# Weight sums behind earlier up tiles on DVE, and every second low half of the product units on POOL

## The chip, the cores and the metric

The kernel runs on one core of a Trainium2 chip. The metric is the device time of one execution in microseconds (us), lower is better. The engines of the core run their own instruction streams and wait for each other by semaphores: TensorE (PE, the matmuls), VectorE (DVE), ScalarE (ACT), GpSimd (POOL), and SyncE (SP), whose queue issues most of the loads from HBM.

## What is computed

Two two-layer transformer-like blocks, one after the other, over 512 tokens of width 1024 in float32 (four layers, 0 to 3). Each layer has mixers and ends with a feed-forward part of inner width 4096, which is where the change is:

```python
h = rms_norm(x, norm_mlp[l])
x = x + jnp.square(jax.nn.relu(h @ w_mlp_in[l])) @ w_mlp_out[l]
```

## The kernel before

**Splits.** Every float32 matmul is made of three on rounded values: a weight unit of 128x1024 (`w_raw`) is copied to `w_hi` by ACT (`split_hi`, L335) in a rounded type, and what is left, `w_lo` = raw - `w_hi`, is subtracted by POOL (`split_lo`, L408) or by DVE (`split_lo_dve`, L356); `by_dve(u)` says which. PE then does `w_hi`·H, `w_lo`·H and `w_hi`·L (L464 to L466). Three slots (`WB` = 3) hold the units in turn, so ACT may split unit u once PE is through with unit u - 3.

**Feed-forward, four blocks of 1024 hidden columns.** Each block has eight *up tiles* (one unit, 24 matmuls of 512 columns each), whose sums lie in two PSUM banks in turn, `acc0` and `acc1`: tile k + 2 can't begin until DVE has evacuated tile k (L723). ACT squares the tile; DVE and ACT then make sums of its quarters (`x_sum`, L730), their rounded halves XH (ACT, L678) and rests XL (`low`, DVE, L736). In blocks 0 to 2 the down projection follows as a *product stage* in Strassen's manner: seven products A11, A12, S1, S4, S2, S3, A22 (`PRODUCTS`), each of two weight units, so units 0 to 13, with 12 matmuls each (L615 to L617; six for the product's tile t = 0, six for t = 1). Their weights are four `quads` of two halves, loaded by SP (`load_quad`, L379), or sums of them, which DVE makes (`w_sum`, L759): two halves each for S1, S3, S2 and A22. S1 and S2 have a place of their own (`w_sums` in the rows), S3 and A22 replace a quad. Block 3 has an ordinary down projection. There are three product stages in each of four layers, twelve in all.

**Taking products.** Each product lies in two PSUM banks and is added to `rows` by DVE when its second unit is done (`take`, L769, one addition each for t = 0 and 1). S4 continues in the banks of S1: PE waits for S1's addition of the same t before unit 6. S2 continues in A11's banks, S3 in S2's, A22 in S3's.

**What sets the order.** Everything is written out by hand in the code's order; each engine works its list in order. For DVE the list is the loop `for k in range(NK)` of `mlp_dve` (tile k: evacuate, sums and rests of x, weight sums, a `w_low`) and the list of `w_low(b, m)`, `take`, `low` and `w_sum` behind it, m being the unit. In the three blocks of layer 0 a `side` function puts some other vector operations behind tile 2 (L1419 to L1429). ACT splits the unit of tile k + 3 when tile k is done, so units 0, 1 and 2 of the stage are split behind tiles 5, 6 and 7.

Of the kernel before, what the change touches and what calls it, by code (L numbers as in the profile page):

```python
# [24 lines left out]
P = 128  # L25
# [4 lines left out]
DEPTH = 2  # L30
HD = 64
EPS = 1e-6
UNIT = 1024
# [57 lines left out]
HALVES = 2  # L91
# [2 lines left out]
W_QUAD = dict(A11=0, A12=1, S4=3, S3=2, A22=1)  # L94
W_EXTRA = dict(S1=0, S2=1)
W_SUM = dict(S1=0, S3=2, S2=4, A22=6)
X_SUM = dict(S3=0, S1=1, S2=2, S4=3)
BY_PAIR = ("A11", "A12", "S1", "S4")
SPLITS = 4 * len(BY_PAIR) + 3
# [3 lines left out]
MULS = HALVES * len(PRODUCTS)  # L103


def taken_after(name):

    return HALVES * (PRODUCTS.index(name) + 1)


def split_after(name, pair):
# [43 lines left out]
def mul_of(u):  # L155

    layer, _, group, _, _, _ = UNITS[u]
    if not group.startswith("mul"):
        return None
    b = int(group[3:])  # L160
    return layer * (FB - 1) + b, u - FIRST_MUL[layer, b]


RANK = []
# [10 lines left out]
def program(nc, given, out):  # L175
# [5 lines left out]
    with ctx:  # L181
# [155 lines left out]
        def by_dve(u):  # L337


            layer, j, group, _, _, _ = UNITS[u]  # L340
            return mul_of(u) is not None or (layer < DEPTH and j >= 2 and group in ("first_in", "late_in"))

        def wait_lo(eng, u):
            mine = by_dve(u)
            eng.wait_ge(lo_split_dve if mine else lo_split, sum(by_dve(x) == mine for x in range(u + 1)))
# [21 lines left out]
        def load_quad(layer, b, q):  # L367


            if b:  # L370
                before, g = FIRST_MUL[layer, b - 1], layer * (FB - 1) + b - 1
                wait_lo(sp, before + {0: 1, 3: 7, 2: 11, 1: 13}[q])
                if q in (0, 3):
                    sp.wait_ge(w_summed, 4 * HALVES * g + (2 if q == 0 else 6))
            elif q == 0:
                n = FIRST_TILE[layer, "out"] + NK - 1
                sp.wait_ge(acc_ready[n % 2], n // 2 + 1)
            for half in range(HALVES):
                sp.dma_start(quads[:, q, half, :],  # L379
                             (w1_in if layer < DEPTH else w2_in)[layer % DEPTH, QUADS_AT[layer, b] + HALVES * q + half, :, :])\  # L380
                    .then_inc(quad_loaded[q], 16)
# [6 lines left out]
        def load_weights(layer):  # L388


            for u, unit in enumerate(UNITS):
                if unit[0] == layer and u >= 2 and mul_of(u) is None:
                    load_unit(u)
                    for b in range(FB - 1):
                        if unit[2] == f"up{b}":
                            at = unit[5] - FIRST_TILE[layer, f"up{b}"]
                            for q in ({1: (0, 3, 2, 1)} if b else {3: (0,), 4: (2,), 5: (3,), 6: (1,)}).get(at, ()):
                                load_quad(layer, b, q)
                if unit[0:2] == (layer, 12) and layer + 1 < LAYERS:
                    load_vec(layer + 1)  # L400

        def split_lo(layer):
            for u, (of, _, _, nk, ntile, _) in enumerate(UNITS):
                if of != layer or by_dve(u):
                    continue
                w, raw = nk * ntile * P, w_raw[:, RANK[u] % 2, 0:nk * ntile * P]
                pool.wait_ge(hi_split, u + 1)
                pool.tensor_tensor(w_lo[:, u % WB, 0:w], raw, w_hi[:, u % WB, 0:w], ALU.subtract)\  # L408
                    .then_inc(lo_split, 1)
# [185 lines left out]
        def products_pe(g, layer, b, XH, XL):  # L595


            for i, name in enumerate(PRODUCTS):
                for half in range(HALVES):
                    pe.wait_ge(x_low, SPLITS * g + split_after(name, 2 * half + 1))  # L600
                    u = FIRST_MUL[layer, b] + HALVES * i + half
                    wait_lo(pe, u)
                    for t in range(2):
                        if half == 0 and name not in OPENS:
                            before = [x for x in PRODUCTS[:i] if PRODUCT_BANK[x] == PRODUCT_BANK[name]][-1]
                            pe.wait_ge(product_taken, MULS * g + taken_after(before) - 1 + t)
                        elif half == 0 and g:
                            before = [x for x in PRODUCTS if PRODUCT_BANK[x] == PRODUCT_BANK[name]][-1]
                            pe.wait_ge(product_taken, MULS * (g - 1) + taken_after(before) - 1 + t)
                        for kk in range(2):  # L610
                            k, c = 2 * half + kk, slice(t * P, t * P + P)
                            xh, xl = XH[:, X_SLOT[name], k, c], XL[:, X_SLOT[name], k, c]
                            wh, wl = w_hi[:, u % WB, kk * T:kk * T + T], w_lo[:, u % WB, kk * T:kk * T + T]
                            bank, ends = product_bank(name, t)[:, :], half == HALVES - 1 and kk == 1
                            pe.matmul(bank, xh, wh, start=(name in OPENS and k == 0), stop=False, skip_group_check=True)  # L615
                            pe.matmul(bank, xl, wh, start=False, stop=False, skip_group_check=True)  # L616
                            last = pe.matmul(bank, xh, wl, start=False, stop=ends, skip_group_check=True)  # L617
                        if half == HALVES - 1:
                            last.then_inc(product_ready, 1)
                        elif t == 1:  # L620
                            last.then_inc(mul_used, 1)
# [94 lines left out]
        def mlp_dve(layer, midH, midL, XH, XL, mid, rows, spare, y, sq, side=None):  # L716
# [22 lines left out]
            def w_low(b, m):  # L739
                if by_dve(FIRST_MUL[layer, b] + m):  # L740
                    split_lo_dve(FIRST_MUL[layer, b] + m)
# [16 lines left out]
                    dve.wait_ge(w_summed, n)  # L758
                dve.tensor_tensor(into, first, second, ALU.subtract).then_inc(w_summed, 1)  # L759

            def take(g, name):
                half, n = PRODUCT_TO[name]
                for t in range(2):
                    at = MULS * g + taken_after(name) - 2 + t
                    dve.wait_ge(product_ready, MULS * g + HALVES * PRODUCTS.index(name) + t + 1)
                    if at:
                        dve.wait_ge(product_taken, at)
                    into = rows[:, 2 * half + t, n * T:n * T + T]
                    dve.tensor_tensor(into, product_bank(name, t)[:, :], into, ALU.add).then_inc(product_taken, 1)  # L769

            for b in range(FB - 1):
                g = layer * (FB - 1) + b
                ups = Group(layer, f"up{b}")
                for k in range(NK):
                    ups.evacuate(part, 1)
                    pair = k // 2
                    if side and k == 2:
                        side((0, 1, 5)[b])
                    if k % 2 == 0:
                        x_sum(g, "S3", pair, "A11", "A21", ALU.subtract)  # L780
                        low(g, "A11", pair)
                    else:
                        x_sum(g, "S1", pair, "A21", "A22", ALU.add)
                        low(g, "A12", pair)
                        x_sum(g, "S2", pair, "S1", "A11", ALU.subtract)
                        x_sum(g, "S4", pair, "A12", "S2", ALU.subtract)
                        if k == NK - 1:
                            w_low(b, 2)
                        low(g, "S1", pair)
                        low(g, "S4", pair)  # L790
                    for name, half in {4: (("S1", 0),), 5: (("S1", 1), ("S3", 0)), 6: (("S3", 1), ("S2", 0))}.get(k, ()):
                        w_sum(g, b, name, half)
                    if k in (5, 6):
                        w_low(b, k - 5)
                w_low(b, 3)
                w_sum(g, b, "S2", 1)
                take(g, "A11")
                w_low(b, 4)
                low(g, "S2")
                w_low(b, 5)  # L800
                w_sum(g, b, "A22", 0)
                w_low(b, 6)
                take(g, "A12")
                take(g, "S1")
                w_low(b, 7)
                low(g, "S3")
                w_low(b, 8)
                w_sum(g, b, "A22", 1)
                w_low(b, 9)
                take(g, "S4")  # L810
                w_low(b, 10)
                take(g, "S2")
                w_low(b, 11)
                low(g, "A22")
                w_low(b, 12)
                take(g, "S3")
                w_low(b, 13)
                take(g, "A22")
# [1942 lines left out]
```

## Time and profile before

| | us |
|---|---|
| median of 3 runs | 3726.57 |
| lowest and highest run | 3726.5, 3732.81 |
| the profiled execution, its own time | 3722.24 |
| its span, first to last instruction | 3720.9 |

The page gives busy time of each engine, the chain of work that ended last, and groups of instructions with the idle time before them; the timelines give single instructions in order of time.

### The profile page before, as it was taken

How to read it: one execution, taken by the hardware profiler on the slowest of the kernel's cores; microseconds unless marked ns; L12 is line 12 of the kernel's file. 1: busy time of each engine (PE TensorE's matmuls, PEld its weight loads, DVE VectorE, ACT ScalarE, POOL GpSimd, SP SyncE). 2: the span in 40 equal slices, each digit the busy share in tenths (PEclk: the TensorE clock that was granted, in tenths of full speed). 3: DMA queues.
4: the chain of work that ended last, by engine and by line, in shares of the span. 5: the costliest groups of instructions: out<-in, count | busy, mean ns of one | idle time of the engine just before them, and what ended most of it. 6: DMA issues, size and time to landing. Idle time of an engine off the chain costs nothing.

```text
span 3720.9 us, 44944 instructions
## 1 busy us (share of the span) xinstructions
PE 3555.5 (96%) x17332; PEld 2727.8 (73%) x17332; DVE 2376.9 (64%) x3416; ACT 1581.1 (42%) x2654; POOL 963.2 (26%) x390
## 2 busy tenths in 40 slices
PE   8889999988999999999999999999999999999998
PEld 6547778854777877577777677787667777777777
DVE  6987777788777754523463687775543355368774
ACT  6464442546444333544333444422444433444442
POOL 0003223100322342132323232244123232332223
PEclk9999999999999999999999999999999999999999
DMA  4103222310322241021212232224112221223312
GB/s 134 43 12 119 91 91 69 93 50 12 115 95 91 63 149 59 29 80 56 80 62 72 61 130 91 80 90 146 41 46 71 65 76 61 69 74 125 114 57 80
DMA packets 80803, 291.94 MB, mean 78 GB/s; under 512 B 9648, under 2 KB 11088, under 8 KB 80080
## 3 DMA queue, kind: packets, MB, share of 16 engines
q1 hardware_dynamic: 77808, 278.03, 23.8%
q10 hardware_dynamic: 2784, 11.03, 0.9%
q8 instruction: 139, 2.28, 0.2%
q14 instruction: 72, 0.59, 0.1%
HBM read 284.84 MB, written 2.10 MB: 77 GB/s over the span
## 4 chain that ended last, share of the span: by engine, by line
PE 76%; DVE 17%; issue 4%; ACT 3%; DMA 0%; DVEq 0%; SPq 0%; ACTq 0%
PE acc L464 18%; PE acc L466 17%; PE acc L465 17%; DVE w_lo L356 3%; PE banks L615 2%; PE banks L616 2%; PE banks L617 2%; PE banks L921 2%; PE banks L970 2%; PE banks L1300 2%; PE banks L953 2%; DVE rows L769 1%; DVE quads L759 1%; DVE w_sums L759 1%; PE banks L2084 1%
## 5 line engine op out<-in xcount | busy, mean ns | idle before, releaser
L408 POOL TENSOR_TENSOR w_lo<-w_raw,w_hi 128x1024 fp32r<-128x1024 f32 x386 | 963.0, 2497 | 2730.9 <-ACT w_hi L335 2730.8
L335 ACT ACTIVATE w_hi<-w_raw 128x1024 fp32r<-128x1024 f32 x422 | 447.5, 1061 | 1080.7 <-PE acc L466 890.6
L464 PE MATMUL acc<-hH,w_hi 128*128 128x512 f32 x1776 | 729.1, 411 | 11.9 <-DVE sig L2472 6.6
L466 PE MATMUL acc<-hL,w_hi 128*128 128x512 f32 x1776 | 699.5, 394 | 0.0
L465 PE MATMUL acc<-hH,w_lo 128*128 128x512 f32 x1776 | 699.1, 394 | 0.0
L464 PEld LDWEIGHTS acc<-hH,w_hi 128*128 128x128 f32 x1776 | 338.1, 190 | 97.6 <-issue 26.3
L464 PE MATMUL acc<-H,w_hi 128*128 128x512 f32 x1024 | 403.2, 394 | 3.8 <-DVE L L528 3.8
L466 PE MATMUL acc<-L,w_hi 128*128 128x512 f32 x1024 | 399.0, 390 | 0.0
L465 PE MATMUL acc<-H,w_lo 128*128 128x512 f32 x1024 | 398.6, 389 | 0.0
L466 PEld LDWEIGHTS acc<-hL,w_hi 128*128 128x128 f32 x1776 | 337.4, 190 | 73.3
L465 PEld LDWEIGHTS acc<-hH,w_lo 128*128 128x128 f32 x1776 | 338.1, 190 | 68.1 <-issue 4.8
L615 PE MATMUL banks<-w_hi,XH 128*128 128x512 f32 x672 | 264.5, 394 | 32.0 <-DVE rows L769 12.8
L616 PE MATMUL banks<-w_hi,XL 128*128 128x512 f32 x672 | 261.9, 390 | 0.0
L617 PE MATMUL banks<-w_lo,XH 128*128 128x512 f32 x672 | 261.8, 390 | 0.0
L464 PEld LDWEIGHTS acc<-H,w_hi 128*128 128x128 f32 x1024 | 192.3, 188 | 45.3 <-DVE L L528 5.5
L466 PEld LDWEIGHTS acc<-L,w_hi 128*128 128x128 f32 x1024 | 192.3, 188 | 40.3
L465 PEld LDWEIGHTS acc<-H,w_lo 128*128 128x128 f32 x1024 | 192.4, 188 | 40.0 <-issue 1.0
L335 ACT ACTIVATE w_hi<-quads 128x1024 fp32r<-128x1024 f32 x120 | 127.3, 1061 | 164.6 <-PE banks L617 96.7
L615 PEld LDWEIGHTS banks<-w_hi,XH 128*128 128x128 f32 x672 | 126.1, 188 | 72.7 <-issue 46.1
L2472 DVE TENSOR_TENSOR sig<-acc,rstd 128x512 f32<-128x512 f32 x48 | 33.2, 691 | 207.1 <-PE acc L466 206.8
L1057 DVE TENSOR_REDUCE stat<-banks 128x1 f32<-128x512 f32 (+2 forms) x192 | 95.8, 541 | 107.5 <-PE banks L928 74.8
L2386 DVE TENSOR_TENSOR Z<-acc,rstd 128x512 f32<-128x512 f32 x80 | 55.2, 689 | 169.3 <-PE acc L466 169.3
(365 smaller groups left out, 5973.4 us busy)
## 6 DMA issues: line engine op xcount, KB each, us to landing
w_raw<-in_stream SPq DMA_DIRECT2D x422, 512.0 KB, 3.6
quads<-in_stream SPq DMA_DIRECT2D x96, 512.0 KB, 4.5
cw<-in_cmpw ACTq DMA_DIRECT2D x2, 2048.0 KB, 7.2
mixed<-in_cmpw ACTq DMA_DIRECT2D x2, 2048.0 KB, 12.6
x_tok<-in_x SPq DMA_DIRECT2D x2, 1024.0 KB, 7.4
out<-probsT SPq DMA_DIRECT2D x4, 512.0 KB, 4.0
stack<-Z ACTq DMA_DIRECT2D x8, 128.0 KB, 2.3
stack<-Z ACTq DMA_DIRECT2D x8, 127.8 KB, 2.5
```

The costliest lines, as they stand in the source:

```text
L335: act.activation(w_hi[:, u % WB, 0:w], raw, ACT.Copy).then_inc(hi_split, 1)
L356: dve.tensor_tensor(w_lo[:, u % WB, 0:w], raw, w_hi[:, u % WB, 0:w], ALU.subtract)\
L408: pool.tensor_tensor(w_lo[:, u % WB, 0:w], raw, w_hi[:, u % WB, 0:w], ALU.subtract)\
L464: pe.matmul(acc[n % 2][:, :], wh, H[:, k, :], start=(k == 0), stop=False)
L465: pe.matmul(acc[n % 2][:, :], wl, H[:, k, :], start=False, stop=False)
L466: last = pe.matmul(acc[n % 2][:, :], wh, Lo[:, k, :], start=False, stop=(k == nk - 1))
L615: pe.matmul(bank, xh, wh, start=(name in OPENS and k == 0), stop=False, skip_group_check=True)
L616: pe.matmul(bank, xl, wh, start=False, stop=False, skip_group_check=True)
L617: last = pe.matmul(bank, xh, wl, start=False, stop=ends, skip_group_check=True)
L759: dve.tensor_tensor(into, first, second, ALU.subtract).then_inc(w_summed, 1)
L921: last = pe.matmul(self.score_banks[h % 3][:, 0:m], w["q"][r, qt * P:(qt + 1) * P], w["k"][r, lo * P:hi * P], start=True, stop=True, skip_ ...
L1057: dve.tensor_reduce(top, bank, AX_X, ALU.max, negate=True).then_inc(up(self.max_ready), 1)
```

## The change

Three things change, in all twelve blocks with a product stage.

1. `by_dve` now gives DVE only the even product units; POOL subtracts `w_lo` of units 1, 3, 5, ... 13, with the same operands.
2. The weight sums stand elsewhere in DVE's list: `W_SUM_AT` puts S1's two halves behind the evacuation of tile 2, S3's first behind tile 3, S3's second and S2's first behind tile 4, and S2's second behind tile 6, in each case ahead of that tile's `x_sum`. Before, they stood at the end of tiles 4 (S1), 5 (S1, S3) and 6 (S3, S2), and S2's second behind `w_low(b, 3)`. A22's second half moves from before `w_low(b, 9)` to behind `take(g, "S4")`.
3. DVE takes A12's first half, S1's first, A12's second, S1's second, where it took both halves of A12 and then both of S1. `taken_after(name, t)` counts in that order.

With them SP's waits ahead of a quad's load name both halves' subtractions, and in a layer's first block the quads are loaded behind tiles 3 (two quads), 4 and 5 where it was 3, 4, 5 and 6.

```diff
+W_SUM_AT = {2: (("S1", 0), ("S1", 1)), 3: (("S3", 0),), 4: (("S3", 1), ("S2", 0)), 6: (("S2", 1),)}
-def taken_after(name):
-    return HALVES * (PRODUCTS.index(name) + 1)
+TAKEN = [("A11", 0), ("A11", 1), ("A12", 0), ("S1", 0), ("A12", 1), ("S1", 1)]
+TAKEN += [(name, t) for name in ("S4", "S2", "S3", "A22") for t in range(2)]
+def taken_after(name, t):
+    return TAKEN.index((name, t)) + 1
...
@@ by_dve
-            return mul_of(u) is not None or (layer < DEPTH and j >= 2 and group in ("first_in", "late_in"))
+            if mul_of(u) is not None:
+                return mul_of(u)[1] % HALVES == 0
+            return (layer < DEPTH and j >= 2 and group in ("first_in", "late_in"))
@@ load_quad
-                wait_lo(sp, before + {0: 1, 3: 7, 2: 11, 1: 13}[q])
+                for half in range(HALVES):
+                    wait_lo(sp, before + {0: 0, 3: 6, 2: 10, 1: 12}[q] + half)
@@ load_weights
-                            for q in ({1: (0, 3, 2, 1)} if b else {3: (0,), 4: (2,), 5: (3,), 6: (1,)}).get(at, ()):
+                            for q in ({1: (0, 3, 2, 1)} if b else {3: (0, 2), 4: (3,), 5: (1,)}).get(at, ()):
@@ split_lo (POOL)
-                w, raw = nk * ntile * P, w_raw[:, RANK[u] % 2, 0:nk * ntile * P]
+                if mul_of(u) is None:
+                    w, raw = nk * ntile * P, w_raw[:, RANK[u] % 2, 0:nk * ntile * P]
+                else:
+                    m = mul_of(u)[1]
+                    w, raw = UNIT, mul_raw(of, PRODUCTS[m // HALVES], m % HALVES)
@@ mlp_dve
+                    for name, half in W_SUM_AT.get(k, ()):
+                        w_sum(g, b, name, half)
                     if k % 2 == 0:
                         x_sum(g, "S3", pair, "A11", "A21", ALU.subtract)
...
-                    for name, half in {4: (("S1", 0),), 5: (("S1", 1), ("S3", 0)), 6: (("S3", 1), ("S2", 0))}.get(k, ()):
-                        w_sum(g, b, name, half)
                     if k in (5, 6):
                         w_low(b, k - 5)
                 w_low(b, 3)
-                w_sum(g, b, "S2", 1)
                 take(g, "A11")
...
-                take(g, "A12")
-                take(g, "S1")
+                take(g, "A12", (0,))
+                take(g, "S1", (0,))
+                take(g, "A12", (1,))
+                take(g, "S1", (1,))
                 w_low(b, 7)
                 low(g, "S3")
                 w_low(b, 8)
-                w_sum(g, b, "A22", 1)
                 w_low(b, 9)
                 take(g, "S4")
+                w_sum(g, b, "A22", 1)
                 w_low(b, 10)
```

Three places of DVE's list show it, in the last product block of layer 1 (its other blocks read alike); the lines of the changed kernel lie some 12 further down (L723, L730, L736, L759, L356, L769 are L735, L742, L748, L771, L363, L781). L723 is a tile's evacuation, L730 a sum and L736 a rest of x, L759 a weight sum, L356 a `w_lo`, L769 an addition. DVE before, from the evacuation of tile 2 to that of tile 4:

```order
L723 SCALAR_TENSOR_TENSOR hidden<-acc,rstd 128x512
L730 TENSOR_TENSOR yt<-hidden 128x256
L736 TENSOR_TENSOR XL<-hidden,XH 128x256
L723 SCALAR_TENSOR_TENSOR hidden<-acc,rstd 128x512
L730 TENSOR_TENSOR hidden<-hidden 128x256
L736 TENSOR_TENSOR XL<-hidden,XH 128x256
L730 TENSOR_TENSOR hidden<-hidden 128x256 x2
L736 TENSOR_TENSOR XL<-hidden,XH 128x256 x2
L723 SCALAR_TENSOR_TENSOR hidden<-acc,rstd 128x512
```

And the same stretch of the changed kernel:

```order
L735 SCALAR_TENSOR_TENSOR hidden<-acc,rstd 128x512
L771 TENSOR_TENSOR w_sums<-quads 128x1024 x2
L742 TENSOR_TENSOR yt<-hidden 128x256
L748 TENSOR_TENSOR XL<-hidden,XH 128x256
L735 SCALAR_TENSOR_TENSOR hidden<-acc,rstd 128x512
L771 TENSOR_TENSOR quads<-quads 128x1024
L742 TENSOR_TENSOR hidden<-hidden 128x256
L748 TENSOR_TENSOR XL<-hidden,XH 128x256
L742 TENSOR_TENSOR hidden<-hidden 128x256 x2
L748 TENSOR_TENSOR XL<-hidden,XH 128x256 x2
L735 SCALAR_TENSOR_TENSOR hidden<-acc,rstd 128x512
```

Three weight sums now stand ahead of the x sums of tiles 2 and 3. The second place, DVE before, from the evacuation of tile 6 to the last rests of tile 7:

```order
L723 SCALAR_TENSOR_TENSOR hidden<-acc,rstd 128x512
L730 TENSOR_TENSOR yt<-hidden 128x256
L736 TENSOR_TENSOR XL<-hidden,XH 128x256
L759 TENSOR_TENSOR quads<-quads 128x1024
L759 TENSOR_TENSOR w_sums<-quads,w_sums 128x1024
L356 TENSOR_TENSOR w_lo<-quads,w_hi 128x1024
L723 SCALAR_TENSOR_TENSOR hidden<-acc,rstd 128x512
L730 TENSOR_TENSOR hidden<-hidden 128x256
L736 TENSOR_TENSOR XL<-hidden,XH 128x256
L730 TENSOR_TENSOR hidden<-hidden 128x256 x2
L356 TENSOR_TENSOR w_lo<-quads,w_hi 128x1024
L736 TENSOR_TENSOR XL<-hidden,XH 128x256 x2
```

And in the changed kernel:

```order
L735 SCALAR_TENSOR_TENSOR hidden<-acc,rstd 128x512
L771 TENSOR_TENSOR w_sums<-quads,w_sums 128x1024
L742 TENSOR_TENSOR yt<-hidden 128x256
L748 TENSOR_TENSOR XL<-hidden,XH 128x256
L735 SCALAR_TENSOR_TENSOR hidden<-acc,rstd 128x512
L742 TENSOR_TENSOR hidden<-hidden 128x256
L748 TENSOR_TENSOR XL<-hidden,XH 128x256
L742 TENSOR_TENSOR hidden<-hidden 128x256 x2
L363 TENSOR_TENSOR w_lo<-quads,w_hi 128x1024
L748 TENSOR_TENSOR XL<-hidden,XH 128x256 x2
```

One weight sum stands there in place of two, ahead of tile 6's x sum, and the `w_lo` of unit 1 is gone to POOL; the one of unit 2 is still last but one. The third place, DVE before at the stage's begin, from the `w_lo` of unit 3 to the additions of A12 and S1:

```order
L356 TENSOR_TENSOR w_lo<-quads,w_hi 128x1024
L759 TENSOR_TENSOR w_sums<-quads,w_sums 128x1024
L769 TENSOR_TENSOR rows<-banks,rows 128x512 x2
L356 TENSOR_TENSOR w_lo<-w_sums,w_hi 128x1024
L736 TENSOR_TENSOR XL<-hidden,XH 128x1024
L356 TENSOR_TENSOR w_lo<-w_sums,w_hi 128x1024
L759 TENSOR_TENSOR quads<-quads,w_sums 128x1024
L356 TENSOR_TENSOR w_lo<-quads,w_hi 128x1024
L769 TENSOR_TENSOR rows<-banks,rows 128x512 x4
```

And in the changed kernel, from the additions of A11 on:

```order
L781 TENSOR_TENSOR rows<-banks,rows 128x512 x2
L363 TENSOR_TENSOR w_lo<-w_sums,w_hi 128x1024
L748 TENSOR_TENSOR XL<-hidden,XH 128x1024
L771 TENSOR_TENSOR quads<-quads,w_sums 128x1024
L363 TENSOR_TENSOR w_lo<-quads,w_hi 128x1024
L781 TENSOR_TENSOR rows<-banks,rows 128x512 x4
```

The `w_lo` of units 3 and 5 and S2's sum are gone from it. The four additions at the end read alike, but their order is A12, S1, A12, S1.

## Rows read from the trace of the kernel before

**Rows 1.** The page: busy time by engine, the last chain, costliest groups.

```profile
PE 3555.5 (96%) x17332; PEld 2727.8 (73%) x17332; DVE 2376.9 (64%) x3416; ACT 1581.1 (42%) x2654; POOL 963.2 (26%) x390
...
PE 76%; DVE 17%; issue 4%; ACT 3%; DMA 0%; DVEq 0%; SPq 0%; ACTq 0%
...
L615 PE MATMUL banks<-w_hi,XH 128*128 128x512 f32 x672 | 264.5, 394 | 32.0 <-DVE rows L769 12.8
```

**Rows 2.** PE's timeline: start us, duration us, engine, line; idle before and releaser bracketed.

```profile
465.36 0.47 PE L615 MATMUL banks<-w_hi,XH 128*128 128x512 f32 x1 [2.50 <-DVE w_lo L356]
...
1075.19 0.39 PE L464 MATMUL acc<-H,w_hi 128*128 128x512 f32 x1
...
1118.71 0.39 PE L615 MATMUL banks<-w_hi,XH 128*128 128x512 f32 x1
...
1121.88 0.47 PE L615 MATMUL banks<-w_hi,XH 128*128 128x512 f32 x1 [0.29 <-DVE w_lo L356]
...
1126.01 0.47 PE L615 MATMUL banks<-w_hi,XH 128*128 128x512 f32 x1 [1.13 <-issue]
...
1138.26 0.47 PE L615 MATMUL banks<-w_hi,XH 128*128 128x512 f32 x1 [1.07 <-DVE rows L769]
...
1160.12 0.39 PE L464 MATMUL acc<-H,w_hi 128*128 128x512 f32 x1
```

**Rows 3.** DVE's timeline, layer 0 block 1, then layer 1 block 1.

```profile
434.05 4.22 DVE L1424 SCALAR_TENSOR_TENSOR sin<-cos,sin 128x512 f32<-128x512 f32 x3
...
1092.18 0.68 DVE L723 SCALAR_TENSOR_TENSOR hidden<-acc,rstd 128x512 f32<-128x512 f32 x1
...
1097.15 0.69 DVE L723 SCALAR_TENSOR_TENSOR hidden<-acc,rstd 128x512 f32<-128x512 f32 x1 [1.22 <-PE acc L466]
...
1108.03 0.69 DVE L723 SCALAR_TENSOR_TENSOR hidden<-acc,rstd 128x512 f32<-128x512 f32 x1
...
1112.28 1.22 DVE L759 TENSOR_TENSOR w_sums<-quads 128x1024 f32<-128x1024 f32 x1
...
1115.88 0.68 DVE L723 SCALAR_TENSOR_TENSOR hidden<-acc,rstd 128x512 f32<-128x512 f32 x1
...
1118.05 1.22 DVE L759 TENSOR_TENSOR quads<-quads 128x1024 f32<-128x1024 f32 x1
...
1120.52 1.22 DVE L356 TENSOR_TENSOR w_lo<-quads,w_hi 128x1024 fp32r<-128x1024 f32 x1
1121.65 0.69 DVE L723 SCALAR_TENSOR_TENSOR hidden<-acc,rstd 128x512 f32<-128x512 f32 x1
...
1124.69 1.22 DVE L356 TENSOR_TENSOR w_lo<-quads,w_hi 128x1024 fp32r<-128x1024 f32 x1
...
1135.84 3.08 DVE L769 TENSOR_TENSOR rows<-banks,rows 128x512 f32<-128x512 f32 x4
```

**Rows 4.** POOL's timeline: 128x1024 subtractions.

```profile
330.84 2.81 POOL L408 TENSOR_TENSOR w_lo<-w_raw,w_hi 128x1024 fp32r<-128x1024 f32 x1 [2.63 <-ACT w_hi L335]
...
1087.47 2.40 POOL L408 TENSOR_TENSOR w_lo<-w_raw,w_hi 128x1024 fp32r<-128x1024 f32 x1 [2.44 <-ACT w_hi L335]
...
1156.09 5.25 POOL L408 TENSOR_TENSOR w_lo<-w_raw,w_hi 128x1024 fp32r<-128x1024 f32 x2 [49.89 <-ACT w_hi L335]
```

**Rows 5.** DVE's timeline beside POOL's operations of rows 4, and one without.

```profile
330.71 0.69 DVE L528 TENSOR_TENSOR L<-yt,H 128x512 fp32r<-128x512 f32 x1
331.31 2.89 DVE L536 TENSOR_TENSOR pair<-pair 128x512 f32<-128x512 f32 x1
...
1087.95 2.21 DVE L730 TENSOR_TENSOR hidden<-hidden 128x256 f32<-128x256 f32 x1 [0.98 <-ACT hidden L692]
...
1109.70 0.43 DVE L730 TENSOR_TENSOR hidden<-hidden 128x256 f32<-128x256 f32 x1 [0.98 <-ACT hidden L692]
...
1158.96 0.69 DVE L769 TENSOR_TENSOR rows<-banks,rows 128x512 f32<-128x512 f32 x1 [2.26 <-PE banks L617]
```

**Rows 6.** ACT's timeline: the split of product unit 2.

```profile
1118.97 1.06 ACT L335 ACTIVATE w_hi<-quads 128x1024 fp32r<-128x1024 f32 x1 [1.29 <-PE acc L466]
```

More of the change, by code:

```diff
@@ L605, in products_pe @@
                             before = [x for x in PRODUCTS[:i] if PRODUCT_BANK[x] == PRODUCT_BANK[name]][-1]
-                            pe.wait_ge(product_taken, MULS * g + taken_after(before) - 1 + t)
+                            pe.wait_ge(product_taken, MULS * g + taken_after(before, t))
                         elif half == 0 and g:
                             before = [x for x in PRODUCTS if PRODUCT_BANK[x] == PRODUCT_BANK[name]][-1]
-                            pe.wait_ge(product_taken, MULS * (g - 1) + taken_after(before) - 1 + t)
+                            pe.wait_ge(product_taken, MULS * (g - 1) + taken_after(before, t))
                         for kk in range(2):
@@ L759, in w_sum, with take @@
                 dve.tensor_tensor(into, first, second, ALU.subtract).then_inc(w_summed, 1)
-            def take(g, name):
+            def take(g, name, ts=(0, 1)):
                 half, n = PRODUCT_TO[name]
-                for t in range(2):
-                    at = MULS * g + taken_after(name) - 2 + t
+                for t in ts:
+                    at = MULS * g + taken_after(name, t) - 1
                     dve.wait_ge(product_ready, MULS * g + HALVES * PRODUCTS.index(name) + t + 1)
```

## The prediction

> **What bounds the kernel now.** I read the page first: TensorE (PE) is busy 96% of the span, and 76% of the chain that ended last is PE [rows 1]. So only what stops PE counts, and the next view is PE's timeline across a feed-forward block. In the second block of the second layer the eight up tiles run without a stop: 192 matmuls from 1075.19 to 1118.71 us, 0.2267 us each [rows 2]. The product stage has 168, which at that pace take 38.09 us, but it runs from 1118.71 to 1160.12, 41.41 us [rows 2]. The 3.32 us are three stops: before unit 1 (0.45 us), unit 2 (1.29) and unit 6 (1.22), each a gap over the pace, plus a first matmul after each stop that takes some 0.08 more; the rows show the idle time that PE's own record has beside them (0.29, 1.13 and 1.07) [rows 2]. PE idled 2.49 us by these records, and the page has 32.0 for the line of a unit's first matmul over all twelve stages [rows 1]: eleven like this one (27.4) and that of layer 0, block 1, which waits 2.50 before unit 1 [rows 2], 2.2 more. The ceiling of any change here is therefore 11 x 3.3 + 5.5 = 42 us.
>
> Who is late is read from DVE's timeline of the same stretch. Unit 1 waits for its w_lo (1120.52 + 1.22 = 1121.74) and unit 2 for its own (1124.69 + 1.22 = 1125.91), and both stand behind weight sums, two from 1112.28 on and two from 1118.05 on [rows 3]. The evacuation of tile 7, ready at 1118.97 when ACT starts on the same signal [rows 6], is at 1121.65 [rows 3]: DVE enters the stage 2.7 us late. Unit 6 needs the bank of S1's first half, taken as the third of four additions that start at 1135.84 [rows 3]: 1135.84 + 3 x 0.79 = 1138.1, and PE goes on at 1138.26.
>
> **The change, part by part.** (1) Of 14 w_lo subtractions in a stage, seven leave DVE, where one costs 1.22 us (1.14 in a row, since the next begins before the last is over) [rows 3], and go to POOL, where one costs 2.40 [rows 4]. DVE is relieved of 7 x 1.14 = 8.0 us, POOL gets 16.8 in a stretch in which it idled for 49.89 [rows 4]. (2) Five of six sums come two to three tiles earlier, S2's last stands behind tile 6 (was: in the stage), A22's second behind the additions of S4. (3) The additions of A12 and S1 alternate, so S1's first is second and not third in line: 0.79 us. (4) Two quads' loads of a layer's first block are issued earlier, and SP waits for each half's subtraction. Nothing is added to PE or ACT.
>
> *The price of part 1.* POOL and DVE exclude each other. The 128x256 pair operation, 0.43 us elsewhere, took 2.21 at 1087.95 [rows 5], and ended 0.29 us behind POOL's of 1087.47 to 1089.87 [rows 4]. The other way round POOL's operation of 330.84 took 2.81 and not 2.40 [rows 4]: it began beside a DVE operation that ended at 331.40; then POOL went first and DVE's next, queued since 331.31, took 2.89, where the one before it, of the same size, took 0.69 [rows 5]. So a waiting POOL gets in at the first boundary between DVE operations, and DVE then loses the whole 2.4. An addition from PSUM isn't held: the one at 1158.96 took 0.69 with POOL at work [rows 4, 5]. The Trainium skill says so too (SBUF — State Buffer, "SBUF: two separate sides"): whichever of the two starts first holds the shared port pair for its whole instruction, DVE only where it has two SBUF inputs or a 2-port mode. By that rule the trade is a bad one, 16.8 us of holding for 8.0 of relief.
>
> *Is there room?* After the change DVE has in a stage 5 subtractions, 3 XL and 2 sums (10 x 1.14 = 11.4) and 14 additions (at most 0.79 each, 11.1): 22.5 us. Six POOL operations that fall in it hold it 14.4 at most: 36.9, under the 38.1 that PE needs even if nothing overlapped, and additions do overlap. Only the moments decide, so I walk this block with the durations above, the same start, and the order of the changed program.
>
> Tiles. Behind the evacuation of tile 2 (1092.18, ends 1092.86) the first sum runs to 1094.0. POOL wanted to start at 1092.9, gets in, and ends at 1096.3; the second sum ends at 1097.35, x_sum and low follow, and tile 3 is evacuated at 1097.96, where it was 1097.15 with 1.22 us of idle before [rows 3]. Behind tile 3 the sum is held by POOL until 1100.7 and ends at 1101.8; tile 4 comes at 1104.2, 1.1 later than it did. Behind tile 4 the first sum delays POOL, POOL holds the second to 1109.4, tile 5 comes at 1110.0 (was 1108.03 [rows 3]). Its accumulator is needed by tile 7 at 1113.2: 2.6 us to spare over its end. Then the lateness turns: no sums stand behind tile 5 (before: two, 2.4 us), tile 6 comes at 1115.05 (was 1115.88 [rows 3]). POOL subtracts unit 1 from 1114.7 to 1117.4, four us ahead of need, and holds S2's sum until 1118.6. Tile 7 comes at 1119.1 instead of 1121.65, 2.5 us earlier.
>
> Stage. Unit 1 is ready and unit 2's w_lo ends at 1122.27 + 1.22 = 1123.5, due at 1124.15: **both stops go** (1.9 us with their restarts). ACT, done with tile 7, splits unit 3 at 1122.7, POOL ends it at 1126.4, due 1126.87: it holds by 0.4. From then on an odd unit has room: ACT begins when the unit three before ends [rows 6], plus 1.06 and 0.08, plus 2.40, is 3.55 us of the 5.44 that two units take. Unit 6 keeps a stop: XL of S2 is wanted at 1129.2, POOL has unit 5 from 1128.3 to 1130.7, so XL ends at 1131.75, A22's sum at 1132.9, w_lo of unit 6 at 1134.0; A12's addition, then S1's from 1134.74 to 1135.43; with 0.12 to PE unit 6 starts at 1135.55 against 1135.04 due, and its second half waits 0.14 for S1's second addition. That is 0.65 plus two restarts of 0.08: the stage takes 38.09 + 0.81 = 38.9 us, **2.5 less**. Later additions meet DVE idle or POOL away (it works from an odd unit's start + 1.1 to the next even one's + 0.8; the two SBUF operations of a pair of units fit before).
>
> Layer 0 has more on DVE behind its tiles 2: in block 1 three operations that took 4.22 us, POOL's hold included [rows 3], in blocks 0 and 2 less. There the two sums add to a queue that is late already. The same walk with these operations put in leaves unit 2 a stop of 0.8, 1.4 and 0.65 us in the three blocks, and in block 1 tile 7 waits 0.3 for tile 5's evacuation and unit 1 0.25 for its XL, too. Against 1.3, 1.3 + 2.7 and 1.3 for those units before, and with unit 6 as above, they gain 1.4, 2.6 and 1.8 us.
>
> Loads cost nothing: quads go out as soon as their units are subtracted, and POOL has unit 13 two units ahead of need, without the two additions that DVE put before it. The sum: 9 x 2.5 + 1.4 + 2.6 + 1.8 = **28.3 us**. The profiled execution took 3722.24, so 3693.9; the median of the runs shown lies 4.3 higher, at 3726.57, which makes **3698** on their scale.
>
> **Rivals.** (A) The walk holds: 3698, chance 0.60.
> (B) The lock bites deeper than walked. If POOL's operations came 10% longer or DVE's 2 to 3%, units 2 and 3 stop again for 0.4 to 0.9 us, since their margins are 0.6 and 0.4, and delays behind tiles 3 to 5 reach tile 6. For it: DVE is busy without a break from tile 2 to tile 6. Then a stage saves 1.2 to 1.9: 3704 to 3713; chance 0.20.
> (C) Stop at unit 6 vanishes as well, because DVE reaches A12's additions a little sooner than walked (0.5 us are enough): 12 x 0.8 = 10 more, 3688; chance 0.10.
> (D) No change to speak of: the walk's order is right but POOL's hold falls on every XL and w_lo that a unit waits for, some 3 us a stage. For it stand the 2.21 and 2.89 us of two short operations [rows 5]; against it that even laid end to end the work fits. 3720 to 3728; 0.05. (The Trainium skill's rule on the shared port pair, cited above, would speak for this case.)
> (E) Slower: POOL doesn't get in between two DVE operations queued back to back, and odd units come late. An odd unit has 5.44 - 3.55 - 0.12 = 1.8 us of room, one and a half DVE operations. From a wait of two (2.3 us) on it stops PE for 0.5 + 0.08, seven times a stage: 38.9 + 4.1 = 43.0, 1.6 more than now, and twelve times that is 19 us: 3745. The row at 330.84 speaks against it, though it is a single one with short operations. 0.05.
>
> Hence the range 3686 (C, and 2 us for scatter) to 3713 (B's end), which leaves out D and E and little of C. A change is told from none here at about 0.2%, 7 us, that is under 3719 or over 3734: faster 0.90 (A, B and C), same 0.05, slower 0.05.
>
> **What the profile would show.** PE's gaps before units 1 and 2 gone in nine stages and smaller in layer 0's; one of about 0.5 before unit 6; stages of 38.9 us; weight sums behind tiles 2, 3 and 4 that take 3.2 us each where POOL is at work; tile 7 evacuated within 0.2 us of being ready; seven POOL operations a stage of 2.4 to 2.8. I am wrong if POOL's w_lo ends later than 4 us behind its ACT split, if sums behind tile 4 push tile 5 past 1112.5, or if PE stops at a tile outside of layer 0.

## The result and the profile after

The changed kernel takes 3702.93 us (median of four runs, 3701.61 to 3705.76) against 3726.64 (3726.5 to 3732.81): 0.9933 of the time, with a 95% interval of 0.9916 to 0.9951. It is 23.7 us faster (18 to 31 by the interval); forecast were 28.3. The profiled execution took 3702.71, with a span of 3701.4.

The page of the changed kernel: busy time, the chain that ended last, and the group of a product unit's first matmuls (L615 is L627 now).

```profile
PE 3560.8 (96%) x17332; PEld 2732.0 (74%) x17332; DVE 2338.0 (63%) x3332; ACT 1581.1 (43%) x2654; POOL 1188.3 (32%) x474
...
PE 82%; DVE 12%; issue 3%; ACT 2%; DMA 0%; SPq 0%; DVEq 0%; ACTq 0%
...
L627 PE MATMUL banks<-w_hi,XH 128*128 128x512 f32 x672 | 264.4, 393 | 6.3 <-DVE rows L781 3.7
```

PE's part of the chain rises from 76 to 82% and DVE's falls from 17 to 12; the idle time before a unit's first matmul falls from 32.0 us to 6.3 [rows 1]. PE's timeline: the stages of layer 0, blocks 0 and 1 (unit 2), then layer 1, block 1, whose stage starts at 1119.41.

```profile
387.79 0.47 PE L627 MATMUL banks<-w_hi,XH 128*128 128x512 f32 x1 [0.60 <-DVE w_lo L363]
...
472.33 0.47 PE L627 MATMUL banks<-w_hi,XH 128*128 128x512 f32 x1 [1.21 <-issue]
...
1119.41 0.39 PE L627 MATMUL banks<-w_hi,XH 128*128 128x512 f32 x1
...
1136.28 0.47 PE L627 MATMUL banks<-w_hi,XH 128*128 128x512 f32 x1 [0.38 <-DVE rows L781]
...
1158.29 0.39 PE L476 MATMUL acc<-H,w_hi 128*128 128x512 f32 x1
```

This stage has one stop of note, 0.54 us over the pace before unit 6 (and 0.11 in the middle of it), and takes 1158.29 - 1119.41 = 38.88 us (41.41 in [rows 2]). So do all of layers 1 to 3, with 38.88 to 38.92, but one of 39.26, where the second half of unit 6 waits 0.39 us more; layer 0's take 39.73, 40.70 and 39.56. DVE's timeline of the same block:

```profile
1093.49 4.55 DVE L771 TENSOR_TENSOR w_sums<-quads 128x1024 f32<-128x1024 f32 x2
...
1099.24 3.30 DVE L771 TENSOR_TENSOR quads<-quads 128x1024 f32<-128x1024 f32 x1
...
1106.82 3.23 DVE L771 TENSOR_TENSOR w_sums<-quads,w_sums 128x1024 f32<-128x1024 f32 x1
...
1110.65 0.68 DVE L735 SCALAR_TENSOR_TENSOR hidden<-acc,rstd 128x512 f32<-128x512 f32 x1
...
1115.73 0.69 DVE L735 SCALAR_TENSOR_TENSOR hidden<-acc,rstd 128x512 f32<-128x512 f32 x1
...
1119.76 0.68 DVE L735 SCALAR_TENSOR_TENSOR hidden<-acc,rstd 128x512 f32<-128x512 f32 x1
...
1122.94 1.22 DVE L363 TENSOR_TENSOR w_lo<-quads,w_hi 128x1024 fp32r<-128x1024 f32 x1
...
1129.87 2.59 DVE L748 TENSOR_TENSOR XL<-hidden,XH 128x1024 fp32r<-128x1024 f32 x1 [1.68 <-ACT XH L690]
1132.39 1.21 DVE L771 TENSOR_TENSOR quads<-quads,w_sums 128x1024 f32<-128x1024 f32 x1
1133.52 1.21 DVE L363 TENSOR_TENSOR w_lo<-quads,w_hi 128x1024 fp32r<-128x1024 f32 x1
1134.66 3.07 DVE L781 TENSOR_TENSOR rows<-banks,rows 128x512 f32<-128x512 f32 x4
```

Both sums behind tile 2 take 4.55 us together, the one behind tile 3 3.30, the second behind tile 4 3.23, where one takes 1.22 alone [rows 3]. Tile 5 is evacuated at 1110.65 and tile 7 at 1119.76; against the stage's start these are 0.05 us from the walk. The `w_lo` of unit 2 stands at 1122.94. POOL's timeline shows the other side:

```profile
1093.61 3.35 POOL L420 TENSOR_TENSOR w_lo<-w_raw,w_hi 128x1024 fp32r<-128x1024 f32 x1 [3.04 <-ACT w_hi L340]
...
1105.56 3.42 POOL L420 TENSOR_TENSOR w_lo<-w_raw,w_hi 128x1024 fp32r<-128x1024 f32 x1 [4.10 <-ACT w_hi L340]
...
1124.51 2.61 POOL L420 TENSOR_TENSOR w_lo<-quads,w_hi 128x1024 fp32r<-128x1024 f32 x1 [6.43 <-ACT w_hi L340]
1128.97 2.41 POOL L420 TENSOR_TENSOR w_lo<-w_sums,w_hi 128x1024 fp32r<-128x1024 f32 x1 [1.86 <-ACT w_hi L340]
```

An operation that DVE's sum got ahead of takes 3.35 and 3.42 us; unit 5's, from 1128.97 to 1131.38, is what holds the XL at 1129.87 for 2.59 us.

**Where the other 4 us are.** For every kernel I took from PE's timeline the start of each block's first matmul and of the first one behind its stage, and added up the twelve blocks (eight up tiles and the stage). Before they take 1029.7 us, after 1001.8: 27.9 less, 28.3 forecast. The rest of the span, which the change doesn't touch, is 3720.9 - 1029.7 = 2691.2 us in the profiled execution of before and 3701.4 - 1001.8 = 2699.6 in this one, so 8.4 more, and the two executions are only 19.5 us apart. Most of the 8.4 is there in the windows of both traces over stretches that come ahead of the first changed instruction: length, busy time of PE, PEld, DVE, ACT and POOL, granted clock, DMA. Before:

```profile
19.00:110.00 91.00, 87.33 (x393) 70.62 (x394) 70.71 (x99) 53.85 (x81) 2.49 (x1) 1.00 0.27 82
110.00:230.00 120.00, 98.93 (x658) 64.44 (x657) 110.69 (x146) 58.81 (x118) 7.64 (x3) 0.96 0.11 36
230.00:340.00 110.00, 102.51 (x451) 65.07 (x450) 76.71 (x112) 63.75 (x121) 22.43 (x9) 0.98 0.18 58
```

And after:

```profile
19.00:110.00 91.00, 87.41 (x379) 69.99 (x380) 68.55 (x96) 52.63 (x79) 2.51 (x1) 0.93 0.27 82
110.00:230.00 120.00, 99.20 (x645) 65.59 (x643) 106.73 (x136) 55.32 (x108) 7.65 (x3) 0.93 0.12 36
230.00:340.00 110.00, 102.97 (x455) 64.29 (x456) 77.25 (x120) 65.45 (x126) 21.82 (x8) 0.98 0.13 41
```

Column PEclk is 1.00 and 0.96 before, and 0.93 twice after. Block 0 of layer 0 begins at 329.45 us before and at 335.72 after: 6.3 us lost where the two programs are the same. Of the other 2.1 us, 2.7 are lost between layer 0's blocks and layer 1's (granted clock 0.98 before, 0.97 after), 1.6 are won between layer 1's and layer 2's, and 1.1 are lost behind the last block. Inside the twelve blocks the granted clock is 1.00 in both traces, so the 27.9 us hold nothing of the clock. The profiled execution of before had a mean clock of 0.991, the highest of all its runs.

### The profile page after: what moved, and what is told of

Read it like the earlier page. It is cut to its first block, busy times and chain, and to the rows that moved or that the text cites. A ratio compares the mean times of both kernels' runs of the same rounds, so it can differ in the third digit from the quotient of the medians.

```text
span 3701.4 us, 44960 instructions
## 1 busy us (share of the span) xinstructions
PE 3560.8 (96%) x17332; PEld 2732.0 (74%) x17332; DVE 2338.0 (63%) x3332; ACT 1581.1 (43%) x2654; POOL 1188.3 (32%) x474
## 4 chain that ended last, share of the span: by engine, by line
PE 82%; DVE 12%; issue 3%; ACT 2%; DMA 0%; SPq 0%; DVEq 0%; ACTq 0%
PE acc L476 19%; PE acc L478 18%; PE acc L477 18%; PE banks L627 3%; PE banks L629 3%; PE banks L628 3%; PE banks L934 2%; PE banks L983 2%; PE banks L1313 2%; PE banks L966 2%; DVE QK L1226 1%; DVE w_lo L363 1%; PE banks L2097 1%; DVE stat L1070 1%; PE banks L1330 1%
## 5 line engine op out<-in xcount | busy, mean ns | idle before, releaser
L420 POOL TENSOR_TENSOR w_lo<-w_raw,w_hi 128x1024 fp32r<-128x1024 f32 x386 | 977.7, 2534 | 2157.2 <-ACT w_hi L340 2157.2
L627 PE MATMUL banks<-w_hi,XH 128*128 128x512 f32 x672 | 264.4, 393 | 6.3 <-DVE rows L781 3.7
L420 POOL TENSOR_TENSOR w_lo<-quads,w_hi 128x1024 fp32r<-128x1024 f32 x60 | 152.5, 2541 | 262.9 <-ACT w_hi L340 262.9
L781 DVE TENSOR_TENSOR rows<-banks,rows 128x512 f32<-128x512 f32 x168 | 116.0, 690 | 111.6 <-PE banks L629 106.2
```

## The experiments

"Blocks" below is that sum of twelve. A walk is what the prediction did for one block: both engines' lists gone through in order, with the trace's durations; the last column has what the expectation on record got from it with the experiment's order put in (where it was put against the changed kernel, counted from that one's 28.3). e9_after_again is the changed kernel. The runs of before beside them had medians of 3730.73 (e1 to e4), 3730.93 (e5 to e8) and 3726.49 (e9 and e10).

| kernel | median | blocks | blocks, against before | expected |
|---|---|---|---|---|
| before | 3729.05 of 25 | 1029.7 | | |
| changed kernel | 3703.25 of 9 | 1001.8 | -27.9 | -28.3 |
| e1_sums: part 2 alone | 3703.88 | 1005.1 | -24.6 | -25 |
| e2_pool: part 1 alone | 3769.61 | 1071.9 | +42.2 | +26 |
| e3_takes: part 3 alone | 3719.29 | 1022.1 | -7.6 | -7 |
| e4_sums_takes: parts 2 and 3 | 3697.92 | 998.6 | -31.1 | -32 |
| e5_late_a22 | 3691.30 | 992.7 | -37.0 | -37 |
| e6_allpool | 3754.19 | 1054.3 | +24.6 | +23 |
| e7_spread | 3700.74 | 998.4 | -31.3 | -32 |
| e8_pool57 | 3691.08 | 988.2 | -41.5 | -42 |
| e10_pool57_again | 3688.86 | 988.5 | -41.2 | -41 |

**Each part alone.** Theory 1: the order of DVE's list pays, the move to POOL doesn't. Theory 2: DVE had too much to do, and what POOL takes off it pays.

e1_sums keeps `W_SUM_AT` and the quads' loads and undoes the rest:

```diff
-                return mul_of(u)[1] % HALVES == 0
+                return True
-TAKEN = [("A11", 0), ("A11", 1), ("A12", 0), ("S1", 0), ("A12", 1), ("S1", 1)]
+TAKEN = [("A11", 0), ("A11", 1), ("A12", 0), ("A12", 1), ("S1", 0), ("S1", 1)]
...
-                take(g, "S1", (0,))
                 take(g, "A12", (1,))
+                take(g, "S1", (0,))
```

> Part 2 of the change alone: the weight sums and quad loads as in the changed kernel, all 14 w_lo subtractions on DVE, additions in the old order. Theory 1 (the order pays, the move to POOL does not): units 1 and 2 lose their stops, unit 6 keeps one of 1.1 us, a stage takes 39.2 us, 25 us less than before in all, about 3701. Theory 2 (DVE had too much work, and the 8 us that POOL takes off it are what pays): with all 14 subtractions on DVE unit 2 or 3 stops again; a stage takes 40.5, 10 us less in all, about 3716.

Measured: 0.993 [0.9916, 0.9945] of before, stages of 39.3 us in layers 1 to 3. PE's timeline has one stop in layer 1, block 1, 1.11 us over the pace before unit 6:

```profile
1134.83 0.47 PE L627 MATMUL banks<-w_hi,XH 128*128 128x512 f32 x1 [0.95 <-DVE rows L781]
```

The sums' places alone give 24.6 of the 27.9 us; with all subtractions on DVE units 1 and 2 don't stop in layers 1 to 3 (in layer 0 unit 2 still does, for 0.27, 1.15 and 0.20 us). Theory 2 has no room. The quads' earlier loads went with the sums and were not run alone, but only a layer's first block has them, and its stage gains no more (41.35 to 39.3 us) than the two behind it (41.41 to 39.3).

e2_pool keeps `by_dve` and POOL's part, and puts sums, loads and additions back:

```diff
-W_SUM_AT = {2: (("S1", 0), ("S1", 1)), 3: (("S3", 0),), 4: (("S3", 1), ("S2", 0)), 6: (("S2", 1),)}
+W_SUM_AT = {4: (("S1", 0),), 5: (("S1", 1), ("S3", 0)), 6: (("S3", 1), ("S2", 0))}
...
                 w_low(b, 3)
+                w_sum(g, b, "S2", 1)
```

> Part 1 of the change alone: odd units' w_lo on POOL, sums and additions in the old places. Theory 1 (order pays, and POOL holds DVE for 2.4 us each time): POOL's units 1 and 3 hold DVE's sums behind tile 6 and in the stage; stops of 2.9 us before unit 2 and 2.0 before unit 4, a stage of 43.6 us against 41.4, 26 us more in all, about 3753. Theory 2 (relief pays): w_lo of unit 1 is ready in time and unit 2's comes 1.1 us earlier: 39.9 us a stage, 18 us less in all, about 3708.

Measured: 1.0105 [1.0088, 1.0121], 39 us slower than the runs of before beside it; theory 2, which had 18 us less, is out. The stage of layer 1, block 1 takes 44.58. DVE's timeline behind tiles 5 to 7, then POOL's:

```profile
1133.81 1.22 DVE L771 TENSOR_TENSOR quads<-quads 128x1024 f32<-128x1024 f32 x1
1134.95 3.42 DVE L363 TENSOR_TENSOR w_lo<-quads,w_hi 128x1024 fp32r<-128x1024 f32 x1
1138.29 0.68 DVE L735 SCALAR_TENSOR_TENSOR hidden<-acc,rstd 128x512 f32<-128x512 f32 x1
...
1145.97 1.22 DVE L363 TENSOR_TENSOR w_lo<-quads,w_hi 128x1024 fp32r<-128x1024 f32 x1
```

```profile
1134.89 2.40 POOL L420 TENSOR_TENSOR w_lo<-quads,w_hi 128x1024 fp32r<-128x1024 f32 x1 [8.48 <-ACT w_hi L340]
```

POOL starts unit 1 at 1134.89 and DVE's `w_lo` of unit 0, begun 0.06 later, takes 3.42 and ends at 1138.37, so tile 6 is evacuated at 1138.29, unit 2's `w_lo` ends at 1147.19, and PE stops for 2.76 us before unit 2:

```profile
1147.29 0.47 PE L627 MATMUL banks<-w_hi,XH 128*128 128x512 f32 x1 [2.76 <-issue]
...
1148.30 0.39 PE L628 MATMUL banks<-w_hi,XL 128*128 128x512 f32 x1
...
1149.32 0.63 PE L628 MATMUL banks<-w_hi,XL 128*128 128x512 f32 x1
...
1151.02 0.63 PE L629 MATMUL banks<-w_lo,XH 128*128 128x512 f32 x1
...
1152.39 0.39 PE L627 MATMUL banks<-w_hi,XH 128*128 128x512 f32 x1
```

The walk had that stop at 2.9. What it didn't have follows in the same rows: from 1148.89 to 1151.88 the matmuls come 0.43 us apart and take 0.63. The windows of this stretch have the granted clock in the column behind POOL's:

```profile
1138.00:1147.00 9.00, 6.53 (x29) 5.07 (x27) 7.35 (x12) 4.38 (x8) 0.00 (x0) 1.00 0.32 117
1147.00:1153.00 6.00, 5.71 (x18) 4.58 (x19) 5.90 (x7) 2.65 (x4) 2.69 (x2) 0.72 0.00 0
1153.00:1184.00 31.00, 29.40 (x131) 24.04 (x130) 21.09 (x22) 13.26 (x13) 17.39 (x7) 1.00 0.33 108
```

It is 1.00 before and behind, and 0.72 from 1147 to 1153, so half of full speed (1.2 of 2.4 GHz) for some 3.4 us. Every stage of this kernel has one such dip: in five it follows unit 2's stop of 2.9 to 3.3 us over the pace, in seven it follows a stop of 2.0 before unit 4, and there the 2.9 before unit 2 had none. A dip costs some 1.6 us, in two stages of layer 0 2.7; in the seven stages it is the whole excess over the expected 43.6 (45.0 to 45.1), and with it the 16 us by which the twelve blocks exceed the walk are accounted for in the main. The length of one stop doesn't tell whether a dip follows. The kernel before has a stop as long, 2.67 us over the pace before unit 1 in layer 0, block 1 [rows 2], and e3_takes has it at 2.65. The windows right behind it, first of before, then of e3_takes, have a granted clock of 1.00 and of 0.72:

```profile
465.00:471.00 6.00, 4.49 (x19) 3.45 (x20) 5.17 (x10) 3.79 (x6) 0.00 (x0) 1.00 0.51 176
```

```profile
465.00:471.00 6.00, 4.08 (x11) 3.30 (x12) 5.17 (x9) 2.62 (x5) 0.00 (x0) 0.72 0.51 167
```

e3_takes has the alternating additions and nothing else: sums, loads and subtractions are those of before.

> Part 3 of the change alone: additions in the order A12, S1, A12, S1, all else as before. Both theories: the stop before unit 6 shrinks by one addition, 0.79 us, and the second half of unit 6 waits 0.14 plus a restart: 0.57 us a stage, 7 us in all, about 3720. If the stop is set by something else than the place in the queue: no change.

Measured: 0.9976 [0.9964, 0.9987], stages of 40.7 to 40.8 but for one of 42.98 in layer 0, the stop before unit 6 0.44 over the pace instead of 1.22. As expected by both.

e4_sums_takes is the changed kernel with `return True` in `by_dve`, so without POOL.

> Parts 2 and 3, without POOL. Theory 1: stops of 0.3 before unit 6 and 0.14 in it, a stage of 38.7 us, 32 us less than before in all and 4 less than the changed kernel: about 3694. Theory 2: slower than the changed kernel by what POOL takes off DVE, stops before units 2 or 3 again, about 3710.

Measured: 0.9915 [0.99, 0.993], stages of 38.65 to 38.69 in layers 1 to 3 but for one of 38.97, and 3.2 us less in the blocks than the changed kernel. PE's one stop in layer 1, block 1:

```profile
1127.56 0.47 PE L627 MATMUL banks<-w_hi,XH 128*128 128x512 f32 x1 [0.15 <-DVE rows L781]
```

0.15 us idle by the record, where the changed kernel has 0.38. Given the sums' places, POOL's part makes the kernel slower: parts 2 and 3 are worth 31.1, and part 1 takes 3.2 of it back.

**What holds unit 6, and POOL's price.**

```diff
@@ e5_late_a22: mlp_dve of the changed kernel
                 w_low(b, 5)
-                w_sum(g, b, "A22", 0)
                 w_low(b, 6)
                 take(g, "A12", (0,))
                 take(g, "S1", (0,))
                 take(g, "A12", (1,))
                 take(g, "S1", (1,))
+                w_sum(g, b, "A22", 0)
```

> The changed kernel with A22's first weight sum moved from before w_lo of unit 6 to behind the additions of A12 and S1. Theory 1 (unit 6's stop is DVE reaching S1's addition late, by the XL of S2 that POOL holds and by the sum behind it): one DVE operation of 1.14 us less ahead of the addition, the stop of 0.54 and the half-unit's 0.14 go; a stage takes 38.1 us in layers 1 to 3, 9 us less than the changed kernel in all. Rival (unit 6 is bound by its w_lo or by something that is not in DVE's list): no change.

Measured: 0.9896 [0.988, 0.9913], stages of 38.08 to 38.13 in layers 1 to 3: not one gap in them. The blocks are 9.1 us shorter than the changed kernel's. It was DVE's list, and one weight sum in it; the rival, no change, is out.

e6_allpool has `return False` for the product units in `by_dve`.

> The changed kernel with all 14 subtractions of a stage on POOL. Theory 1 (each POOL operation shuts DVE's two-input operations out for 2.4 us): POOL is at work nearly all of the stage, DVE's XL and sums wait, stops of 1.7 before unit 1 and 1.4 before unit 3 and 0.2 to 0.5 before the others, a stage of 43 us, 51 us more than the changed kernel in all, plus what a lower clock after the stops costs. Theory 2 (relief of DVE pays): DVE has another 8 us less to do, POOL at 2.40 a unit is under the 2.72 that PE takes for one, so 38.1 a stage, 10 us less than the changed kernel.

Measured: 1.0061 [1.0046, 1.0076], stages of 42.9 to 43.2 us. PE's stops before unit 1 and unit 3:

```profile
1141.82 0.50 PE L627 MATMUL banks<-w_hi,XH 128*128 128x512 f32 x1 [1.64 <-DVE XL L748]
...
1148.82 0.47 PE L627 MATMUL banks<-w_hi,XH 128*128 128x512 f32 x1 [1.26 <-POOL w_lo L420]
```

DVE had 16 us less to subtract in a stage than in the kernel before, and PE stops longer, for a rest of x at unit 1 and for POOL itself at unit 3. That is theory 1 with its number: 52.5 us more than the changed kernel in the blocks, 51 expected. Of these, 46 are in the stages and 6.5 among up tiles of layers 0 and 1 that the walk didn't have waiting. The lower clock that the expectation allowed for didn't show here: the granted clock is 1.00 in all twelve blocks, behind stops of 1.8 and 1.4 us and behind one of 2.4 before tile 7 in layer 0.

e7_spread puts the six sums one behind each tile:

```diff
+W_SUM_AT = {2: (("S1", 0),), 3: (("S1", 1),), 4: (("S3", 0),), 5: (("S3", 1),), 6: (("S2", 0),), 7: (("S2", 1),)}
```

> The changed kernel with the six weight sums one behind each of tiles 2 to 7 (S1, S1, S3, S3, S2, S2). If the 0.6 to 1.4 us that layer 0's units 2 keep come from two sums standing behind tile 2's other work: layer 0's stages get 0.9, 1.7 and 0.5 us shorter, layers 1 to 3 stay at 38.9; 3.5 us less in all. If they come from elsewhere: no change. A sum behind tile 7 that comes too late for unit 2's w_lo would show as a stop of over 1 us in every stage.

Measured: 0.9917 [0.9902, 0.9931]. Layer 0's stages take 38.90, 39.23 and 38.94, so 0.8, 1.5 and 0.6 less than with the changed kernel, and the waits of 0.2 and 0.35 among the up tiles of its first two blocks are gone; the others stay. 3.4 us less in the blocks.

e8_pool57 joins e5 and e7 and leaves POOL two units:

```diff
-                return mul_of(u)[1] % HALVES == 0
+                return mul_of(u)[1] not in (5, 7)
```

> POOL subtracts units 5 and 7 alone, the sums stand one behind each of tiles 2 to 7, and A22's first sum behind the additions of A12 and S1. By the walk nothing stops PE any more: 38.1 us in every stage, 42 us less than before, 14 less than the changed kernel. If POOL's part were the gain, taking five of its seven operations back would cost 5 us and more.

Measured: 0.9891 [0.9873, 0.9909]. The stage of layer 1, block 1, from its first matmul to the first of the next tile, on PE's timeline:

```profile
1115.25 0.39 PE L627 MATMUL banks<-w_hi,XH 128*128 128x512 f32 x1
...
1153.39 0.39 PE L476 MATMUL acc<-H,w_hi 128*128 128x512 f32 x1
```

That is 38.14 us, the pace of 168 matmuls, and all twelve stages are like it (38.08 to 38.14). It beats both kernels. Its median was no better than e5's, though its blocks are 4.5 us shorter: its four runs had clocks of 0.985 to 0.990, and the one at 0.990 took 3682.25.

**Is the rest the clock?** Two kernels were run again, with more runs of before beside them.

> The changed kernel once more, in more rounds. The forecast took 28.3 us off, the medians differ by 23.7, the blocks in the trace by 28.0. If the missing 4 us are the granted clock of single executions (the profiled run of before had 0.991, the changed kernel's 0.987), runs of equal mean clock differ by 28, and medians over more runs by 26 to 30. If they are a cost of the change outside of its blocks, runs of equal clock differ by 24.

> The kernel with POOL at units 5 and 7 alone once more. Its blocks took 986.4 us in the trace against 999.9 of the changed kernel, its median was 3691.1 at clocks of 0.985 to 0.990. If only the clock of single runs hides the rest: 13 us under the changed kernel at equal clock, about 3689 by the median. If a denser PE is granted a lower clock: its clocks lie below those of the changed kernel in these rounds too, and the gap is 9 or less.

(The sums of blocks in these two expectations were counted from a slightly different start than those of the table; their differences are the same within 0.1 us or so.)

Measured: the changed kernel 3703.48 (five runs, 3703.2 to 3705.38, clocks 0.987 and 0.988), 0.9939 [0.9925, 0.9952] of before, whose nine runs beside it had 3726.49. e10_pool57_again took 3688.86 (clocks 0.986 to 0.989), 0.9901 [0.9887, 0.9914]. The 26 to 30 us expected by the medians were not reached (23.0). The 25 runs of before beside the experiments have a median of 3729.05 and a mean clock of 0.9883, the changed kernel's nine 3703.25 and 0.9874: 25.8 us (24.6 with the first four runs of before, whose clocks aren't on record). At a mean clock of 0.988 five runs of before have a median of 3730.93 and four of the changed kernel 3704.6: 26.3 apart; at 0.987 the one run of before took 3733.39, and the median of the changed kernel's five is 3703.20: 30.2. With before's own slope (median 3731.99 at 0.986, 3725.85 at 0.990, so 1.5 us per 0.001) the 0.0009 of clock make 1.4 us, which puts the change at 27.2. The walk's 28.3 and the blocks' 27.9 are right within what this can tell, since the groups at equal clock hold one to five runs; a cost of the change outside of its blocks (24 us at equal clock) fits them less. The denser kernel isn't granted less than the changed one (0.9874 over its eight runs, e8 and e10 together).

## Why the prediction was right, point by point

**The ceiling and who is late.** Right: e8_pool57 has no stop left and its blocks are 41.5 us shorter, the ceiling was 42.

**The price of part 1** (POOL and DVE exclude each other, POOL gets in at the first boundary, an addition from PSUM isn't held). Right, and the sizes too: sums of 3.2 to 3.3 us where 3.2 was forecast; in e2_pool and e6_allpool this exclusion makes PE's stops. Rival E needed POOL to be kept out by queued DVE operations; in the profile after it waits one operation at most (3.42 = 2.40 + 1.02), at both places where DVE has two in a row. The Trainium skill's rule (SBUF — State Buffer, "SBUF: two separate sides"), by which the operation that starts first has the shared ports for its whole length, makes the trade a bad one by the prediction's own count, 16.8 us of holding for 8.0 of relief; e4_sums_takes agrees, 3.2 us are lost by it. The prediction said as much but never walked the change without POOL; that walk, done for e4_sums_takes, gave 4 us more gain. So the time is right although one of the three parts works against it.

**Room and moments.** Right: stages of 38.88 against 38.9; tile 7 on time; unit 3 in time by some 0.45 us; one stop before unit 6, 0.54 where 0.51 was walked, set by the XL of S2 that POOL holds and the sum behind it (e5_late_a22).

**Layer 0.** Forecast were gains of 1.4, 2.6 and 1.8 us in its three blocks, measured are 1.4, 2.6 and 1.85 (with what its up tiles lose). The parts: unit 2's stops were walked as 0.8, 1.4 and 0.65 us and are 0.76, 1.37 and 0.55, and an up tile waits in blocks 0 and 1, where the prediction named one in block 1 alone. The close totals are in part luck: unit 6 stops for 0.3 us and not the 0.51 that it was given here too, and unit 3 stops for 0.12 to 0.15 and a restart of 0.08, which the walk didn't have; the two cancel. e7_spread, where the sums stand one by one, takes unit 2's stops down to 0, 0.19 and 0, so how the sums are packed is the cause; which of its five moved sums does it was not separated.

**The sum.** 28.3 against 27.9 in the blocks. (In reading S1's addition the prediction writes 1135.84 + 3 x 0.79 = 1138.1; it is 1138.2, and nothing rests on it.) What was mis-sized is the last step, from the profiled execution to the median: I took the 28.3 off the median of three as if the rest of the program took equal time in every run. The runs of before vary by some 13 us, and with the granted clock (3722.24 to 3735.64 in the 25 beside the experiments), and in both kernels' first runs the rest took 4 us off the gain. That put the time at 3702.93 and not 3698, nearer to rival B's 3704 than to the walk. The traces decide between them: B needed longer POOL operations and stops before units 2 and 3, and in layers 1 to 3 of the changed kernel there are none. Why the changed kernel's runs all have 0.987 or 0.988, where before has 0.985 to 0.991, stays open: in both of its traces block 0 begins over 6 us late, ahead of the first changed instruction, and e5_late_a22 and e8_pool57, with the same instructions there, reached 0.990. I made no kernel to tell chance from cause.

## What to carry to other kernels

Where an engine issues in order and its list is full for a while, ask of each operation when its result is due, and put what is due late behind what is due soon; here moving seven weight sums and two additions among places where DVE was busy anyway was worth 31 us, and taking half of the subtractions off DVE on top of it cost 3. An operation moved to POOL costs DVE up to the whole of POOL's time (2.40 us here for 1.14 saved), wherever DVE's next work is a two-input operation on SBUF. A walk through one block with the trace's own durations, both engines' order and that exclusion gave every arrangement here but one within 2 us over twelve blocks (the one whose long stops brought a lower clock with them), and it found e8_pool57, which is 14 us better than the change.

## What the runs showed of the hardware that I had not expected

A stop of PE of 2.76 us in the middle of dense work was followed by some 3.4 us at half the clock (granted 0.72 in the window of 1147 to 1153 us of e2_pool), and so, in other stages of that kernel, was one of 2.0. The same stop can come with the dip and without: 2.67 us over the pace in layer 0, block 1 of before had none behind it, 2.65 at that place in e3_takes had one. The stops of 0.4 to 1.3 us in before and of 1.4 to 2.4 in e6_allpool had none. What decides, these runs don't show. And where the clock falls in the first 340 us differs between programs that are alike there: block 0 begins at 329.5 us in the trace of before, at 335.7 and 336.2 in two of the changed kernel, at 331.4 to 333.6 in those of seven experiments and at 336.0 in e8_pool57's, whose repetition began at 333.5.
